# Half of a layer's late modulation vectors computed as row sums on VectorE instead of as small matmuls on TensorE

## What is computed

```python
mod_ctx = jax.nn.silu(c_ctx) @ ada_w[l] + ada_b[l]          # context group
mod = (jax.nn.silu(c) @ ada_w[l] + ada_b[l])[:, None, :]    # latent group
sh1, sc1, g1, sh2, sc2, g2 = jnp.split(mod, N_MOD, axis=-1)
h = _rms_norm(x, lp['norm1_g']) * (1 + sc1) + sh1
proj = h @ lp['w_in']
...                                                          # DeltaNet, latent attention, windowed attention
x = x + g1 * mix
h2 = _rms_norm(x, lp['norm2_g']) * (1 + sc2) + sh2
x = x + g2 * (jnp.square(jax.nn.relu(h2 @ lp['w_ff1'])) @ lp['w_ff2'])
```

## Time and profile before

| | |
|---|---|
| median of 3 runs | 1979.01 us (1978.17 to 1980.53) |
| the profiled execution: its time | 1980.32 us |
| its span, first to last instruction | 1978.5 us |
| mean granted TensorE clock | 0.978 of full |
| TensorE matmul busy | 94% of the span |
| VectorE, ScalarE, GpSimd busy | 53%, 34%, 24% |
| input projection of the first layer | about 44.6 to 273 us |
| median of the three runs less the profiled time | -1.31 us |

### The profile page before, as it was taken

The page is one execution under the profiler, slowest core; times in us unless marked ns, Lnnn a source line. Parts: engine busy times, 40 slices in busy tenths (PEclk is TensorE's granted clock), DMA queues, the critical chain, the costliest instruction groups (busy, mean ns, idle before and its releaser), DMA issues. The chain is left out here.

```text
span 1978.5 us, 32729 instructions
## 1 busy us (share of the span) xinstructions
PE 1863.0 (94%) x14119; PEld 1759.2 (89%) x14119; DVE 1058.4 (53%) x1572; ACT 679.6 (34%) x1044; POOL 468.2 (24%) x334
## 2 busy tenths in 40 slices
PE   5999999887999999999999999888799999999996
PEld 3999976676999999999999997667699999999996
DVE  3455675575744676767655576457574323232323
ACT  2454246522233231322326533652223213132231
POOL 4000010145242040412430001014523304031244
PEclk9999999999999999999999999989999999999998
DMA  8445120101233444444231122010021211221211
GB/s 348 150 150 172 61 86 1 38 1 45 80 118 118 139 138 160 151 148 151 74 139 65 53 78 83 1 38 2 27 96 65 86 65 64 86 85 65 83 46 54
DMA packets 49231, 178.66 MB, mean 90 GB/s; under 512 B 21472, under 2 KB 23264, under 8 KB 32576
## 3 DMA queue, kind: packets, MB, share of 16 engines
q1 hardware_dynamic: 47552, 175.09, 25.1%
q10 hardware_dynamic: 1536, 1.48, 0.2%
HBM read 167.79 MB, written 8.68 MB: 89 GB/s over the span
## 5 line engine op out<-in xcount | busy, mean ns | idle before, releaser
L1459 PE MATMUL PS<-HH,HI 128*128 128x322 f32 (+1 forms) x1792 | 417.7, 314 | 4.5 <-DVE HL L958 4.5
L1459 PE MATMUL PS<-HL,HI 128*128 128x322 f32 (+1 forms) x1792 | 414.7, 313 | 0.0
L1459 PE MATMUL PS<-HH,LO 128*128 128x322 f32 (+1 forms) x1792 | 414.0, 312 | 0.0
L622 ACT CAST HI<-RAW 128x2048 fp32r<-128x2048 f32 x96 | 182.9, 1905 | 492.5 <-PE PS L1459 465.8
L1459 PEld LDWEIGHTS PS<-HH,HI 128*128 128x128 f32 x1792 | 303.3, 190 | 5.1 <-issue 5.0
L1459 PEld LDWEIGHTS PS<-HH,LO 128*128 128x128 f32 x1792 | 305.7, 191 | 0.0
L1459 PEld LDWEIGHTS PS<-HL,HI 128*128 128x128 f32 x1792 | 304.6, 191 | 0.0
L1459 PE MATMUL PS<-FH,HI 128*128 128x320 f32 x1280 | 293.1, 310 | 1.4 <-DVE FLO L1340 1.4
L1459 PE MATMUL PS<-FH,LO 128*128 128x320 f32 x1280 | 291.4, 309 | 0.0
L951 DVE TENSOR_TENSOR LO<-RAW,HI 128x2048 fp32r<-128x2048 f32 x96 | 232.8, 2425 | 101.7 <-ACT HI L622 101.7
L1459 PE MATMUL PS<-FL,HI 128*128 128x320 f32 x1152 | 262.4, 309 | 0.0
(11 more groups left out here) (277 smaller groups left out, 2295.1 us busy)
## 6 DMA issues: line engine op xcount, KB each, us to landing
RAW<-ws SPq DMA_DIRECT2D x96, 1024.0 KB, 4.9
ADA<-ada SPq DMA_DIRECT2D x24, 1024.0 KB, 5.1
WM<-adt SPq DMA_DIRECT2D x48, 512.0 KB, 3.6
X<-xT SPq DMA_DIRECT2D x1, 2560.0 KB, 15.7
X<-xT SPq DMA_DIRECT2D x2, 1280.0 KB, 5.7
xs<-X SPq DMA_DIRECT2D x1, 2560.0 KB, 8.0
X<-xs SPq DMA_DIRECT2D x2, 1280.0 KB, 5.6
yT<-YB SPq DMA_DIRECT2D x8, 320.0 KB, 2.2
```

The source lines that it names most:

```text
L622: nc.scalar.copy(HI[g % 2][:, :], RAW[g % 2][:, :]).then_inc(hi_ready, 1)
L1459: last = pe.matmul(bank(2 * u + a)[:, 0:e], w[:, cols], m[:, a, 0:e], start=(k == 0 and f), stop=(k == KT - 1 and e_))
```

## The change

The 16 chunks on TensorE are divided. `ada`, `ada_row` and `adt` keep only the first 8 (shift of the second norm, gate of the first half). The scale and the gate of the second norm, 2048 values, are made as 16 row-sum tiles on VectorE, in slots 2 to 12: two each in slots 2, 4, 6, 8 and 10, one in each of the others. Their vector `CBX` and three buffers `WMX` lie where the activations `X` were, which is free once both parts of the norm are made. The shared code of a row-sum tile is now `mod_tile`. ScalarE gets one Silu of `CBX` in slot 1. GpSimd sets `LW` to zero only after the last row-sum tile, since the memory is shared.

```diff
+MOD_IN = {2: 2, 3: 1, 4: 2, 5: 1, 6: 2, 7: 1, 8: 2, 9: 1, 10: 2, 11: 1, 12: 1}
+MF = 16
...
+        CBX = place("CBX", [P, 2, D], F32, r_x)
+        WMX = [place(f"WMX{i}", [P, D], F32, r_x + 8192 + i * 4096) for i in range(3)]
...
                         if s % 2 == 0:
                             refill(g0 + s // 2 + 1)
-                        if l == 0 and 1 <= s <= 14:
+                        if l == 0 and s == 1:
+                            sp.wait_ge(nsq, 15)
+                            sp.wait_ge(S["h_lo"], KT)
+                            sp.dma_start(CBX[:, :, :], t["crow"].partition_broadcast(P)).then_inc(vb_in, 16)
+                            for n in range(3):
+                                sp.dma_start(WMX[n][:, :], t["adt"][n]).then_inc(mw_in[n], 16)
+                        if l == 0 and s in MOD_IN:
+                            first = sum(MOD_IN[x] for x in MOD_IN if x < s)
+                            for n in range(first + 3, min(first + MOD_IN[s] + 3, MF)):
+                                sp.wait_ge(modn, n - 2)
+                                sp.dma_start(WMX[n % 3][:, :], t["adt"][n]).then_inc(mw_in[n % 3], 16)
+                        if l == 0 and 1 <= s <= 6:
                             sp.wait_ge(S["ada_mm"], o["ada_mm"] + s)
                             ada_load(s + 1)
...
                     if l:
                         pool.wait_ge(x_st, 16 * l)
+                    else:
+                        pool.wait_ge(modn, MF)
                     nc.gpsimd.memset(LW[leafs, :, :, :], 0.0).then_inc(S["wi"], 1)
...
                         if j >= 1:
                             tile_out(j - 1)
+                        if l == 0 and j == 1:
+                            act.wait_ge(vb_in, 16)
+                            nc.scalar.activation(CBX[:, :, :], CBX[:, :, :], ACT.Silu).then_inc(silu_c, 1)
...
+                def mod_tile(n, j, w, cond):
+
+                    if n == 0 or n == MF:
+                        dve.wait_ge(silu_c, 3 if n else 2)
+                    dve.wait_ge(mw_in[n % 3], 16 * (n // 3 + 2))
+                    if n:
+                        dve.wait_ge(modn, n)
+
+                    def share(g):
+                        return nc.vector.scalar_tensor_tensor(out=MPR[:, :], in0=w[:, :], scalar=1.0, in1=cond[:, g, :],
+                                                              op0=ALU.mult, op1=ALU.mult, accum_out=MODN[:, j, g:g + 1])
+                    link(share(0))
+                    share(1).then_inc(modn, 1)
...
-                        if l == 0 and 2 <= j <= 17:
+                        if l == 0 and 2 <= j <= 9:
                             ada_row(j - 2)
...
                             if l == 0:
-                                dve.wait_ge(S["ada_tr"], 16)
-                                link(ada_bias(2 * KT, 6 * KT, VEC[:, 2 * KT:6 * KT]))
+                                dve.wait_ge(S["ada_tr"], 8)
+                                dve.wait_ge(modn, MF)
+                                link(ada_bias(2 * KT, 4 * KT, VEC[:, 2 * KT:4 * KT]))
+                                link(row_bias(4 * KT, 6 * KT, VEC))
...
+                        if l == 0 and j in MOD_IN:
+                            first = sum(MOD_IN[x] for x in MOD_IN if x < j)
+                            for n in range(first, first + MOD_IN[j]):
+                                mod_tile(n, 4 * KT + n, WMX[n % 3], CBX)
                         for k in range(*LEAF_STEPS.get(j, (0, 0))):
                             leaf_step(k)
...
-                        if l == 0 and 1 <= j <= 16:
+                        if l == 0 and 1 <= j <= 8:
                             ada(j - 1)
...
-                        if l == 0 and 2 <= j <= 17:
+                        if l == 0 and 2 <= j <= 9:
                             adt(j - 2)
```

More of the change, by code:

```diff
@@ L121 @@
     xtr=4, xa=16, xb=16, xo=4, xhi=8, xlo=8, f1_re=32, f1_hi=32, f1_sq=32, f1_lo=32,
-    ada_mm=16, ada_ev=16, ada_tr=16, mod_done=1, moda_done=2)
+    ada_mm=8, ada_ev=8, ada_tr=8, mod_done=1, moda_done=2)
 def build(nc, t):
@@ L349, in ada_bias, with row_bias @@
                                            vec.unsqueeze(2).broadcast_to([P, hi - lo, 2]), ALU.add)
-        def row_bias(lo, hi):
+        def row_bias(lo, hi, vec):
             return nc.vector.tensor_tensor(MOD[:, lo:hi, :], MODN[:, lo:hi, :],
-                                           VB[:, lo:hi].unsqueeze(2).broadcast_to([P, hi - lo, 2]), ALU.add)
+                                           vec[:, lo:hi].unsqueeze(2).broadcast_to([P, hi - lo, 2]), ALU.add)
         def ada_gain(q, sc, vec):
@@ L397, in next_load @@
                         if j < MT:
+                            n = MF + j
                             if j >= 3:
-                                sp.wait_ge(modn, j - 2)
-                            sp.dma_start(WM[j % 3][:, :], t["adt"][j]).then_inc(mw_in[j % 3], 16)
+                                sp.wait_ge(modn, n - 2)
+                            sp.dma_start(WM[n % 3][:, :], t["adt"][n]).then_inc(mw_in[n % 3], 16)
                     if l == 0:
@@ L737, in _ @@
                             if l == 0:
-                                act.wait_ge(S["ada_tr"], 16)
+                                act.wait_ge(S["ada_tr"], 8)
                             for n, x in enumerate((TCKV[:, :], TCQ[:, 0, :], TCQ[:, 1, :])):
@@ L1129, in _ @@
                             if l == 0:
-                                dve.wait_ge(S["ada_tr"], 16)
-                                link(ada_bias(2 * KT, 6 * KT, VEC[:, 2 * KT:6 * KT]))
+                                dve.wait_ge(S["ada_tr"], 8)
+                                dve.wait_ge(modn, MF)
+                                link(ada_bias(2 * KT, 4 * KT, VEC[:, 2 * KT:4 * KT]))
+                                link(row_bias(4 * KT, 6 * KT, VEC))
                             else:
-                                link(row_bias(2 * KT, 6 * KT))
+                                link(row_bias(2 * KT, 6 * KT, VB))
                             ada_gain(1, 4 * KT, VEC[:, V_N2:V_N2 + KT]).then_inc(S["mod_done"], 1)
@@ L1376, in next_mod @@
                             return
-                        j = MOD_AT[c, part] + e
-                        if j == 0:
-                            dve.wait_ge(silu_c, 2)
-                        dve.wait_ge(mw_in[j % 3], 16 * (j // 3 + 2))
-                        if j:
-                            dve.wait_ge(modn, j)
-                        def share(g):
-                            return nc.vector.scalar_tensor_tensor(out=MPR[:, :], in0=WM[j % 3][:, :], scalar=1.0, in1=CB[:, g, :],
-                                                                  op0=ALU.mult, op1=ALU.mult, accum_out=MODN[:, j, g:g + 1])
-                        link(share(0))
-                        share(1).then_inc(modn, 1)
+                        n = MF + MOD_AT[c, part] + e
+                        mod_tile(n, n - MF, WM[n % 3], CB)
                     q = 2 * l + 1
@@ L1427, in _ @@
                         if c == 2 and l + 1 < DEPTH:
-                            row_bias(0, 2 * KT).then_inc(S["moda_done"], 1)
+                            row_bias(0, 2 * KT, VB).then_inc(S["moda_done"], 1)
                             dve.wait_ge(S["moda_done"], o["moda_done"] + 1)
@@ L1945, in lay_out @@
         "ada": c(tiles(a["ada_w"][0:1], AC).reshape(1, 6 * D // AC, P, KT, AC)),
-        "adt": c(a["ada_w"][1].T.reshape(MT, P, D)),
+        "adt": c(np.concatenate([a["ada_w"][0].T.reshape(MT, P, D)[MT - MF:], a["ada_w"][1].T.reshape(MT, P, D)])),
         "crow": c(np.stack([a["c"][0], a["c_ctx"]]).reshape(2, D)),
```

5 lines of the change are left out of this document (3 added, 2 removed).

## The result

The changed kernel takes **1966.85 us** (median of 5 runs, 1962.86 to 1969.09), and the kernel before, run beside it, 1978.17 (5 runs, 1977.33 to 1980.53). The ratio is **0.9942, interval 0.9929 to 0.9955**: 11.5 us shorter by the ratio, with 8.9 and 14.0 as its ends. The prediction said 1969.9 with a range from 1966.8 to 1975.5, and "faster" at 0.82. The kernel is faster, and by the mechanism that was forecast; the time lies at the low end of the range, and under it, at 1966.7, if the ratio is applied to 1978.17. It is also 3.05 us from the forecast, outside the 2 us given to it, and nearer to the 1967.3 of rival 1 (no stops), though the stops did come. The profiled execution took 1966.85 us, its span 1965.1.

What follows compares the result with a forecast made beforehand. TensorE, 94% busy and never idle in the projection, was taken as the bound: 11.7 us leaving it less 2.6 of stops gives 9.1, so 1980.3 becomes 1971.2, or 1969.9 as median; 8-in-10 range 1966.8 to 1975.5.

Steps and rivals of the forecast that it cites:

- rival 1: Projection: TensorE is never stopped and the full 11.7 us shows, 1967.3 on the median's scale; chance 0.08.
- What bounds the kernel: Projection, 60 to 273 us: TensorE never idles, so each instruction leaving it saves its own time unless VectorE's lateness stops it.
- What leaves TensorE: Tails 9 to 17: removed `ada` and `adt` save about 1.0, 7 x 1.47 and 0.36 us, together 11.7.
- The row-sum tile: VectorE, slots 2 to 12: 2.5 us a tile with both sums and reads, 40 us for 16 tiles.
- the higher price: VectorE: row sums reaching 2.491 us each, about 5 us a tile, seen beside GpSimd's work, which is absent in the projection.
- The stops: Tails 2, 3 and 7: TensorE waits 1.2, 0.7 and 0.6 us for the copy to `MODB`; sum 2.5, booked 2.6.
- The scale of the medians: Whole kernel: 1971.2 us for an execution like the profiled one, the median of runs 1.3 lower, so 1969.9.
- Nothing is given back later: After slot 12: leaf steps begin with no lateness and loads stay covered, so the rest of the kernel is booked at nothing.
- rival 3: End of the projection: TensorE arrives 9 us early and waits for leaf chain or value copies, about 1979 to 1980; chance 0.08.
- Rival 2: Projection: bigger stops (net 6 us) or a clock fall with each of three stops (net 4), 1974 to 1976; chance 0.15.
- Rival 4: Slots 2 to 12: VectorE becomes the bound; 5 us a tile gives net 25 slower, deciding from 3.3; chance 0.07.
- The table load, by row and by page: ScalarE, Silu of `CBX`: 1.30 us from load to Silu by row; the page's 2.66 would make the first stop 2.6, net 7.7.

Runs made afterwards that it cites:

- the repeat: The changed kernel once more, unaltered: 1966.17 us (1962.93 to 1970.84), ratio 0.9947 (0.9934 to 0.9960).
- two small edits: Changed kernel with the Silu of `CBX` in slot 2: 1965.6 us, 0.9939; or with the copy to `MODB` first: 1961.46 us, 0.9922, again 1962.32.
- the repeat of before: The kernel before once more, unaltered, for a second trace: 1979.11 us (one run).

## What held of the prediction, and the step that failed

**What bounds the kernel: right.** Taking work off TensorE shortened the stretch by its full length, 12.74 us by itself and 10.50 with the stops (12.74 - 2.28 = 10.46).

**What leaves TensorE: the step that failed.** The mechanism was right; this term of the sum was mis-sized. Booked 11.7, measured 12.65 (12.74 over the longer stretch). "both cost 1.47 us" was read from the start of `ada` to the start of the row behind `adt`. The last large row ahead of the group and the next small one behind it are longer as well, by 0.09 and up to 0.08. The six slots of tails 10 to 15 gain 9.50 instead of 6 x 1.47 = 8.82, tail 9 gains 1.20 instead of 1.0, tails 16 and 17 gain 1.95 instead of 1.47 + 0.36: together that is the 1.0 us. The price should have been taken between two large matmuls, or from a period: a slot with a pair against one without.

**The row-sum tile: right.** 2.5 us was taken, and two sums of 1.22 and two reads of 0.08 stand in the trace. GpSimd has no instruction while they run; its clearing of `LW` starts at 171.04, behind the last sum. That the higher price belongs to GpSimd's work fits the trace of before, where the two sums from 692.52 to 697.33 take 2.28 and 2.49 us and GpSimd works from 692.04 to 696.25; no run here put GpSimd beside the new tiles to test it.

**The stops: right in place and cause, slightly high in size.** 1.2, 0.7 and 0.6 us in tails 2, 3 and 7 were forecast; the trace has 1.22, 0.65 and 0.25, released by the copies to `MODB`, and none after. The ends of these copies were forecast at 71.8, 81.7 and 120.9, measured 71.88, 81.80 and 120.66. The third stop is smaller because the copy came 0.24 early and TensorE, at 120.10 + 0.39 = 120.49, came 0.2 later than "118.40 + 1.9" has it. In all they cost 2.28 where 2.6 was booked. The two errors point the same way, 1.04 and 0.3, so the net up to tail 18 is 10.5 and not 9.1.

**The scale of the medians.** 1979.01 was the median of before given first, 1978.17 that of the runs beside the changed kernel: 0.8 us. With the 1.4 of the terms, 2.2 of the 3.05 between 1969.9 and 1966.85 are explained. The rest, 0.9, is smaller than the interval of the ratio. That the repeat gives 0.9947, 10.5 us, just the net of the tile times, is luck to the decimal: its interval is 5 us wide.

**Nothing is given back later: right, and rival 3 falls.** The lead is carried through the kernel. The same block of weights (the 56th to be split, in the second layer's projection) on VectorE, before and then after:
```profile
1116.48 2.29 DVE L951 TENSOR_TENSOR LO<-RAW,HI 128x2048 fp32r<-128x2048 f32 x1 [0.97 <-ACT HI L622]
```
```profile
1106.02 2.29 DVE L973 TENSOR_TENSOR LO<-RAW,HI 128x2048 fp32r<-128x2048 f32 x1 [0.97 <-ACT HI L641]
```
10.46 us ahead. That this meets the 10.50 so closely is chance in part, since falls of the clock lie ahead of it in both: with the repeats, at 1115.29 and 1102.33, the lead is between 9.3 and 14.2. The one long wait of TensorE at the end of the projection, for `QKV`, is 1.61 us in all four traces, so nothing new is waited for there. At the last block the two profiled executions are 13.46 apart (1930.27 and 1916.81). The further 3.0 are no effect of the change: from the 56th block to the last it is 813.79 us in before, 813.78 in its repeat and 813.78 in the repeat of after; only the first execution of after has 810.79. It differs between 1200 and 1250 us, where the granted clock is 0.90 before and 0.97 after (0.90 in the repeat of after).
```profile
1200.00:1250.00 50.00, 44.78 (x220) 0.90 0.20 51
```
```profile
1200.00:1250.00 50.00, 44.14 (x272) 0.97 0.15 31
```

**Rival 1, no stops,** is what each of two small edits reaches: 152.00 from tail 1 to 18, 12.74 better than before, where it had 11.7. For the kernel as changed it did not come, though its 1967.3 is the nearest to the measured median.

**Rival 2, the clock answers to the stops,** does not hold for the stops of this change, 0.3 to 1.2 us. The stretch from 62.5 to 216.5 has a granted clock of 1.00 in after:
```profile
62.50:216.50 154.00, 151.88 (x1275) 145.19 (x1275) 124.78 (x209) 78.29 (x102) 2.02 (x2) 1.00 0.44 150
```
With stops up to 4.1 and 5.9 us, in the kernels with more row sums, the first 145 us of this stretch stand at 0.95 and 0.87, one trace of each. The Trainium skill, page "TensorE: Matmul & The Clock Gate", section "What's actually happening", ties the clock to how busy the engine has lately been. For these two kernels the trace agrees. For the falls at full busyness no run here shows such a link; the earlier trace rows is one of them, there in one execution of before and absent in the other.

**Rival 4, VectorE the bound,** did not come. At 3.8 us a tile the kernel is slower than before by 0.28%, so the turning point lies below. A straight line through 154.24 at 2.5 us and 171.32 at 3.8 crosses the 164.74 of before at 3.3 us, the forecast value; that is an estimate, and as the distance rises faster from 3.8 to 5.0 (20.3 us) than from 2.5 to 3.8 (17.1), the true point is rather above it. The forecast reached 3.3 by stops alone, which is luck: by the stops alone the turning point would be 3.8.

**The table load, by row and by page.** The Trainium skill, page "ScalarE: Activation LUTs", section "What ACT_TABLE_LOAD costs", books a drain on top of the load, 2.66 us in all. The trace does not agree: from the table load to the Silu are 63.80 - 62.50 = 1.30 us, the load begins 0.01 behind the end of the output's row (61.47 + 1.02 = 62.49), and the first stop is 1.22 and not 2.6.

## What to carry to other kernels

Price work that leaves a saturated engine by a period, a slot with it against a slot without, never by the distance between its own rows: here its neighbours paid 0.08 to 0.13 us more in each slot. When work is moved to an engine with room, walk its queue slot by slot and ask which copy stands behind it that the saturated engine waits for; that gave three stops to within 0.3 us, and putting that copy first removed all of them. And look at a stretch whose clock did not fall when a few microseconds are compared, since the median carries the clock's wandering as well: gains of 2.2 us that every trace showed were hardly visible in three of five medians.

## What the runs showed of the hardware

A group of small matmuls costs what stands beside it too. The last large row ahead of it takes 0.39 us to the group's start where the group has the form 128*32, and 0.30 where it has 128*128; the ten one-column matmuls on `SQT` take 1.18 us behind `adt` and 1.10 behind a large row.

The granted clock of a kernel that keeps TensorE 94% busy falls at some places that are the same in both executions taken of it and at some that are not, also while TensorE is busy without a gap (225 to 240 us in the repeat of before: 15.00 of 15.00 us busy, 0.77); 41 to 44 us of full clock are lost in each of the four traces of before and after. Where the clock was down ahead of 50 us, in three traces, the projection came no later.

Where TensorE was stopped for several microseconds in one slot after another, the distance grew by half as much again as the stops themselves: 6.7 beside 12.6 us, and 15 beside 24.5, with the granted clock at 0.95 and 0.87.
